# Five buffers of a two-block fp32 transformer kernel begin 32 bytes higher in SBUF

## What is computed

```python
h2 = rms_norm(x, norm2_w[l]) * (1.0 + scale2[:, None]) + shift2[:, None]
f = jnp.square(jax.nn.relu(h2 @ w_ff1[l])) @ w_ff2[l]      # 2048 -> 8192 -> 2048
x = x + gate2[:, None] * f
```

## Time and profile before

| | |
|---|---|
| median of 3 runs | 2521.94 us (2521.39 to 2523.83) |
| profiled execution, span from first to last instruction | 2525.1 us |
| TensorE matmul busy | 2465.1 us (98%), 15316 matmuls |
| TensorE weight loads | 2203.4 us (87%) |
| VectorE / ScalarE busy | 2001.2 us (79%) / 1289.3 us (51%) |
| HBM traffic | 652.16 MB, mean 258 GB/s |
| granted TensorE clock, mean | 0.994 |

### The profile page before, as it was taken

One profiled execution on the slowest core, in us unless ns is written; L12 is line 12 of the kernel. 1 busy time (PEld: TensorE's weight loads), 2 busy tenths in 40 slices (PEclk: granted clock), 3 DMA queues, 4 the chain that ended last, 5 costly groups with the idle time before them and its releaser, 6 DMA issues.

```text
span 2525.1 us, 38356 instructions
## 1 busy us (share of the span) xinstructions
PE 2465.1 (98%) x15316; PEld 2203.4 (87%) x15321; DVE 2001.2 (79%) x2640; ACT 1289.3 (51%) x1883; POOL 4.0 (0%) x11
## 2 busy tenths in 40 slices
PE   6799999999999999999999999999999999999999
PEld 5689999898888888889898888888898888888888
DVE  7979988979986888889968678998778756656655
ACT  5454445555555555555546566554454444444443
POOL 0000000000000000000000000000000000000000
PEclk8999999999999999999999999999999999999999
DMA  9988997767777778778559677888578755555554
GB/s 374 392 303 313 327 347 282 249 227 271 257 264 262 255 252 293 256 258 274 180 192 326 231 278 261 318 318 292 194 252 317 261 187 186 194 187 186 193 189 134
DMA packets 142387, 652.16 MB, mean 258 GB/s; under 512 B 13009, under 2 KB 64209, under 8 KB 77441
## 3 DMA queue, kind: packets, MB, share of 16 engines
q1 hardware_dynamic: 141106, 645.06, 71.9%
q0 software_dynamic: 672, 3.31, 0.3%
q10 hardware_dynamic: 432, 1.35, 0.2%
HBM read 647.58 MB, written 2.10 MB: 257 GB/s over the span
## 4 chain that ended last, share of the span: by engine, by line
PE 85%; DVE 6%; DMA 5%; ACT 2%; issue 2%; SPq 0%; DVEq 0%; ACTq 0%
PE PM L579 44%; PE PM L580 23%; DMA raw<-in_w_in 4%; PE PM L576 3%; PE PM L577 3%; PE PM L578 3%; DVE WL L1240 2%; DVE raw L1247 2%; PE PS L605 2%; PE PS L609 2%; PE PS L606 2%; DMA raw<-in_w_out 1%; PE PS L623 1%; PE PS L624 1%; PE PS L625 1%
## 5 line engine op out<-in xcount | busy, mean ns | idle before, releaser
L874 ACT CAST WH<-raw 128x1024 fp32r<-128x1024 f32 (+1 forms) x881 | 880.9, 1011 | 988.5 <-PE PM L580 654.6
L1240 DVE TENSOR_TENSOR WL<-raw,WH 128x1024 fp32r<-128x1024 f32 (+1 forms) x881 | 1016.5, 1172 | 423.8 <-ACT WH L874 421.9
L579 PE MATMUL PM<-H,WH 128*128 128x512 f32 x2944 | 1027.2, 393 | 0.4 <-DVE WL L1240 0.4
L580 PE MATMUL PM<-H,WL 128*128 128x256 f32 x2944 | 823.1, 280 | 0.0
L579 PEld LDWEIGHTS PM<-H,WH 128*128 128x128 f32 x2944 | 551.3, 187 | 125.4 <-issue 0.7
L580 PEld LDWEIGHTS PM<-H,WL 128*128 128x128 f32 x2944 | 555.6, 189 | 0.1
L1247 DVE CUSTOM_DVE_ANT_0 raw<-raw,cb 128x2048 f32<-128x2048 f32 x192 | 436.9, 2283 | 2.6 <-DMA raw<-in_w_mod 1.6
L579 PE MATMUL PM<-FC,WH 128*128 128x512 f32 x1024 | 358.7, 393 | 0.0
L580 PE MATMUL PM<-FC,WL 128*128 128x256 f32 x1024 | 285.8, 279 | 0.0
L579 PEld LDWEIGHTS PM<-FC,WH 128*128 128x128 f32 x1024 | 191.9, 187 | 45.9
L580 PEld LDWEIGHTS PM<-FC,WL 128*128 128x128 f32 x1024 | 191.9, 187 | 0.0
(11 more groups left out here) (335 smaller groups left out, 3196.1 us busy)
## 6 DMA issues: line engine op xcount, KB each, us to landing
raw<-in_w_ff SPq DMA_DIRECT2D x128, 1024.0 KB, 4.9
raw<-in_w_in SPq DMA_DIRECT2D x112, 1024.0 KB, 6.4
raw<-in_w_mod SPq DMA_DIRECT2D x96, 1024.0 KB, 7.6
raw<-in_w_ada SPq DMA_DIRECT2D x96, 1024.0 KB, 6.3
raw<-in_w_up SPq DMA_DIRECT2D x80, 1024.0 KB, 5.4
raw<-in_w_down SPq DMA_DIRECT2D x64, 704.0 KB, 5.6
raw<-in_w_out SPq DMA_DIRECT2D x16, 1024.0 KB, 7.4
raw<-in_w_o SPq DMA_DIRECT2D x16, 1024.0 KB, 5.6
```

What stands on the lines that cost most here:

```text
L579: PE.matmul(bank(n)[:, :], wh, rhs, start=(kk == 0), stop=False)
L580: return PE.matmul(bank(n)[:, T:2 * T], wl, rhs[:, 0:T], start=False, stop=ends)
L874: S.copy(part(WH), w).then_inc(s_hi, 1)
L1240: V.tensor_tensor(part(WL), w, part(WH).bitcast(F32), ALU.subtract).then_inc(s_lo, 1)
```

## The change

One unused buffer of 8 floats, 32 bytes per partition, is laid out ahead of `FC`. The two `FC`, `gr`, `go` and `xo` move up by 32 bytes, and `FC` then begins at a multiple of 128 bytes (all sizes from `FC` on are multiples of 128 too). No instruction is added, removed or moved, and every other buffer keeps its address.

```diff
--- before.py
+++ after.py
@@ -351,6 +351,7 @@
                 qc = sb("qc", [128, 8], on=att)
                 exact = sb("exact", [128, 3, 128], F32R, att)
             MG = sb("MG", [128, 16, 2 * T], F32R, mix2)
+        sb("gap", [128, 8])
         FC = [sb(f"FC{i}", [128, 16, 2 * T], F32R) for i in range(2)]
         gr = sb("gr", [128, 3, T])
         go = sb("go", [128, 4, T])
```

## The result

The changed kernel takes 2526.7 us (median of 20 runs, 2523.8 to 2529.5) where the one before takes 2521.6 (20 runs beside them): ratio 1.0020, 95% interval 1.0014 to 1.0026. It is 5.0 us slower. The forecast was 3.5 us faster.

A forecast was written before the change was run, and what follows sets the result against it. The prediction took TensorE to be the bound throughout the last stage. FC at H's pace would save 3.51 us, other terms 0, so 2521.94 - 3.5 = 2518.4 us (-0.14%), range 2516.2 to 2523.4.

The forecast's parts named there:

- What bounds the kernel, and the two paces: From 1985.8 us on, TensorE is the bound, in FC and H stretches; FC takes about 350.1 ns a tile, H 346.7.
- The cause: FC's tiles are 3.4 to 3.5 ns slower than H's because FC begins 96 bytes past a multiple of 128.
- the rival on the far side: FC falls into H's other pace, 353.3 ns: 2525.2 us, or 2528.6 with H drawn along; chances 0.09 (or mixed) and 0.04.
- The sum: FC's three stretches at H's pace give back 0.88, 0.89 and 1.74 us, together 3.51, all on the path.
- The stretches of H "are not touched": The H stretches between and behind the FC stretches keep their time; no gain or loss was counted there.
- The disturbance at the entry: At each step from H into FC the third 512-column matmul lasts 0.42 us, not 0.39; uniform alignment would remove it.
- No effect through VectorE, ScalarE, DMA or the tail: Other readers and writers of the moved buffers cost the same; at most 0.02 us after the last matmul, taken as 0.
- The rival of no change: H is fast for a reason other than its offset from a multiple of 128; time stays 2521.9 us; chance 0.21.
- the drawn-along case: The H stretches behind the first two FC stretches also go to 353.3 ns: +3.4 us more, 2528.6; chance 0.04.

The follow-up runs named there:

- the kernel that kept all distances: 32 unused bytes laid out ahead of the first buffer, so every buffer moves alike, against the kernel before the change: 2518.2 us, ratio 0.9983.
- 160 bytes: The unused buffer ahead of FC has 160 bytes instead of the change's 32; against the kernel before the change: 2518.2 us, ratio 0.9989.

## Why the prediction was wrong

*What bounds the kernel, and the two paces.* Right for the last stage. TensorE is busy from 2000 to 2500 us without a gap in all 17 profiles, and 350.1 for FC against 346.7 for H came back there in the kernel that kept all distances.

*The cause.* This step failed. The prediction explained the two paces by the offset from a multiple of 128 bytes. It had two classes of buffers, H and the rest, and they differed in every modulus at once. The weight buffers were noted as aligned too, but only as one more address and not as the thing to measure from. What FC's pace goes by in these runs is the distance from `WH` modulo 256, and the change moves FC from 96 to 128 and not to 0. "H is fast because it shares a finer or a coarser offset with the weights" stood among the rivals, but only with the price of no change: I never worked out what FC at 128 past a coarser boundary would do. The measured 2526.7 lies between the two prices of the rival on the far side (2525.2 and 2528.6) by the sum, and not by its mechanism.

*The sum.* The term of -3.51 us for FC was +1.0 (351.1 for 350.1, 1024 tiles). With 160 bytes the same term came out as predicted, 346.6.

*The stretches of H "are not touched".* Wrong, put at nothing and measured at +3.4 us, the larger part of the loss. (Of the distance to the forecast, FC's term makes up 4.5 us and this one 3.4.) The rival on the far side had exactly this price, 512 x 6.6 ns, but tied it to FC being caught at 353.3 first and gave it 0.04. FC was never at 353.3; it handed on a rhythm at its own 351.1. The argument for the low chance, that H goes 256 tiles without a flip, speaks of jobs within a stretch and not of the step back from FC.

*The disturbance at the entry.* The long third matmul is gone (0.39 at 1984.05 for the 0.42 of the earlier trace rows), as predicted. But it is no sign of a good pace: it went away with FC at 351.1. Nor does it come with every step from H to a buffer at d = 96. With 32 bytes ahead of everything, the first step to FC goes without it (no tile of that stretch takes more than 356 ns from start to start) and the second has one of 388 ns. What brings it is open.

*No effect through VectorE, ScalarE, DMA or the tail.* Nothing in the runs speaks against it. MG at 350.0 ahead of FC held too.

*The rival of no change.* Wrong too. A shift of 32 bytes moved paces by 1.0 (FC, 96 to 128), 6.6 (160 to 192) and, on H, 6.6 ns a tile. The Trainium skill's rule in "SBUF — State Buffer" (note on SBUF "cachelines") speaks of 16-byte lines only; such a shift keeps all their boundaries, so the rule alone doesn't describe this.

*The range* had 2523.4 for its upper end, and "slower" had 0.06. A wider end, to the 2528.6 of the drawn-along case, was what two unseparated explanations deserved.

## What to carry to other kernels

Where TensorE is the bound, compare the start-to-start pace of the same pair of matmuls on each operand buffer; a full busy share hides 2%. If the paces differ, vary the distance of moving operand and weight buffers (and of the two weight buffers from each other) before an absolute alignment, and read every stretch after it too, since a rhythm can be handed on to code that wasn't touched. Profile more than one execution where the times scatter: which pace a stretch has can differ without any distance having changed. When a trace has only two classes of addresses, it can't say which modulus separates them; spread the range over the candidates.

## What the runs showed of the hardware that I had not expected

- The pace of a pair of fp32r matmuls (512 and 256 columns) with a new weight tile each goes by the distance of the moving operand from WH modulo 256. On FC it was 346.7, 350.1, 351.1, 346.7, 353.2 and 353.3 ns at 0, 96, 128, 160, 192 and 224 bytes. That it goes on in steps of 256 rests on 0, 256 and 512, and on two positions of 128; the values at 160, 192 and 224 rest on one profile each.
- At 0 and at 224 two paces exist, 346.7 and 353.3. Each is kept for hundreds of tiles and for the next buffer at the same distance, until something breaks it. A zero matmul turned 353.3 into 346.7 in two experiments and in the earlier trace rows. But a break doesn't always end in 346.7. With 32 bytes between H and the weights the zero matmul of the earlier trace rows leaves H, at d = 224, at 353.3 on both sides. And the zero matmul ahead of the first long stretch of pairs on H (its weight load at 534.11 us before) is followed by 346.7 before, and by 353.3 with 32 bytes ahead of everything.
- With WH and WL 32 or 64 bytes off each other the second pace appeared in none of four profiles. Folded tiles of FB, 360.0 ns before, went to 354.3 with the 32 bytes between WH and WL alone (175 steps in 62.0 us):

```profile
L577 PE MATMUL PM<-FB,WH x176: 274/279/361, 1150.0 to 1212.0; 128*128 128x256 f32 x176
```

What in the chip does this, two read streams that meet in the same part of the memory or something else, no run here shows. Nor did any separate the four `WH` slots, the PSUM banks, or tile shapes other than these two.
